# The latent attention's projection stage: tiles in turn, or a pipeline over three tiles

## The reference

```python
z = h @ lw['w_in']
c_q = rms_norm(z[..., :O_KVL], lw['g_q_lora'])
q = rms_norm(jnp.einsum('bsr,rhd->bshd', c_q, lw['w_uq']), lw['g_mla_qn'])        # 8 heads of 96
q = jnp.concatenate([q[..., :QK_NOPE], apply_rope(q[..., QK_NOPE:], cos, sin)], axis=-1)
latent = jnp.concatenate([rms_norm(z[..., O_KVL:O_KR], lw['g_kv_lora']), z[..., O_KR:O_DIL]], axis=-1)
...
k_nope = jnp.einsum('btr,rhd->bthd', c_kv, w_uk)      # 8 heads of 64
inv = lax.rsqrt((sum(k_nope ** 2) + sum(kr ** 2)) / QK_DIM + EPS)
k_nope = k_nope * (inv[..., None] * g_kn[:QK_NOPE])
kr = apply_rope(kr * g_kn[QK_NOPE:], cos, sin)        # 32 wide, times inv of each head
v = jnp.einsum('btr,rhd->bthd', latent[..., :KV_LORA], lw['w_uv'])
```

## Time and profile before

| | us |
|---|---|
| time, median of 3 executions (lowest to highest) | 4498.88 (4493.37 to 4502.63) |
| span of the profiled execution; no other time of it is recorded | 4461.3 |
| start of the tile loop's first product | 131.32 |
| start of the next stage's first product | 272.77 |
| TensorE busy over the whole span | 3866.2 (87%) |
| VectorE busy over the whole span | 2746.1 (62%) |
| ScalarE busy over the whole span | 1193.5 (27%) |

### The profile page before, as it was taken

One profiled execution on the slowest core, in us unless ns is written; L12 is line 12 of the kernel. 1 busy time (PEld: TensorE's weight loads), 2 busy tenths in 40 slices (PEclk: granted clock), 3 DMA queues, 4 the chain that ended last, 5 costly groups with the idle time before them and its releaser, 6 DMA issues.

```text
span 4461.3 us, 43547 instructions
## 1 busy us (share of the span) xinstructions
PE 3866.2 (87%) x14598; PEld 2550.7 (57%) x14598; DVE 2746.1 (62%) x6469; ACT 1193.5 (27%) x3201; POOL 861.8 (19%) x717
## 2 busy tenths in 40 slices
PE   7789879999995699977999677879999999899986
PEld 5458357798984588865444344434444445454443
DVE  1665535352345311236999997766779766976876
ACT  2356333232222101122222367621111111111111
POOL 0000000100000000001333323333333333343332
PEclk8889869997697599988999889999999999999997
DMA  4000200312114311125888879999999999999997
GB/s 152 5 2 1 55 38 22 117 45 85 60 48 152 105 43 43 62 92 194 310 316 328 326 306 354 384 418 414 413 398 379 414 412 410 373 394 414 389 357 286
DMA packets 252635, 1016.82 MB, mean 228 GB/s; under 512 B 25434, under 2 KB 100594, under 8 KB 167426
## 3 DMA queue, kind: packets, MB, share of 16 engines
q0 software_dynamic: 101520, 723.10, 40.9%
q1 hardware_dynamic: 130722, 280.49, 17.1%
q10 hardware_dynamic: 20176, 10.49, 0.8%
HBM read 964.74 MB, written 49.25 MB: 227 GB/s over the span
## 4 chain that ended last, share of the span: by engine, by line
PE 26%; DVE 15%; DMA 11%; issue 2%; ACT 2%; POOL 0%; SPq 0%; ACTq 0%; DVEq 0%
PE banks L2357 9%; PE banks L2343 8%; DMA ff_room<-in_v 8%; DVE ff_rows L2006 4%; PE banks L2332 4%; PE banks L2280 2%; DVE ff_acc L1972 2%; DMA gates_dram<-ff_room 1%; PE banks L2225 1%; DMA ff_rows<-in_uv,pk_expert 1%; DVE pk_eq L1662 1%; DVE pk_axes L1667 1%; DVE mx_x L2032 1%; PE banks L2304 1%; DVE pk_besti L1641 1%
## 5 line engine op out<-in xcount | busy, mean ns | idle before, releaser
L1904 POOL DMA_INDIRECT ff_rows<-in_uv,pk_expert x640 | 806.0, 1259 | 1507.6 <-DVE ff_acc L1972 828.4
L2006 DVE CUSTOM_DVE_ANT_0 ff_rows<-ff_rows,ff_h_row 128x1024 f32<-128x1024 f32 x648 | 766.4, 1220 | 43.9 <-DMA ff_rows<-in_uv,pk_expert 42.0
L2357 PE MATMUL banks<-ff_room,mx_x 128*128 128x512 f32 x1536 | 703.1, 609 | 59.0 <-DVE mx_x L2047 32.5
L2343 PE MATMUL banks<-mx_x,ff_room 128*128 128x384 f32 x2048 | 683.4, 487 | 10.9 <-ACT mx_x L2190 10.4
L2343 PEld LDWEIGHTS banks<-mx_x,ff_room 128*128 128x128 f32 x2048 | 389.3, 190 | 310.3 <-issue 73.5
L2332 PE MATMUL banks<-ff_rows,o_mla_tops 128*128 128x512 f32 x904 | 445.5, 642 | 138.3 <-ACT o_mla_tops L2100 134.7
L2357 PEld LDWEIGHTS banks<-ff_room,mx_x 128*128 128x128 f32 x1536 | 297.6, 195 | 420.6 <-issue 359.0
L1972 DVE SCALAR_TENSOR_TENSOR ff_acc<-ff_rows,ff_a,ff_acc 128x1024 f32<-128x1024 f32 x388 | 498.6, 1285 | 7.2
L2332 PEld LDWEIGHTS banks<-ff_rows,o_mla_tops 128*128 128x128 f32 x904 | 178.7, 206 | 355.4 <-issue 198.0
L176 PE MATMUL banks<-d_w_high,h_high 128*128 128x512 f32 (+1 forms) x648 | 275.7, 425 | 30.7 <-DVE d_w_low L183 29.8
L2088 ACT ACTIVATE ff_gelu<-ff_dots 128x2 f32<-128x2 f32 x324 | 65.7, 203 | 822.8 <-DVE ff_dots L2006 822.5
(11 more groups left out here) (379 smaller groups left out, 5942.9 us busy)
## 6 DMA issues: line engine op xcount, KB each, us to landing
ff_room<-in_uT SPq DMA_DIRECT2D x128, 512.0 KB
ff_room<-in_v SPq DMA_DIRECT2D x128, 512.0 KB
gates_dram<-ff_room SPq DMA_DIRECT2D x6, 4096.0 KB, 16.6
mx_x<-gates_dram SPq DMA_DIRECT2D x128, 192.0 KB
d_w<-in_w_dil POOLq DMA_DIRECT2D x9, 2048.0 KB, 12.7
d_w<-in_w_ada POOLq DMA_DIRECT2D x32, 512.0 KB, 4.7
ff_room<-in_w_pq SPq DMA_DIRECT2D x32, 512.0 KB
ff_rows<-in_uv,pk_expert POOLq DMA_INDIRECT x640
```

What stands on the lines that cost most here:

```text
L1904: pool.indirect_dma_start(out=rows[r][:, :], out_offset=None, in_=IN["uv"][:, :], in_offset=bass.IndirectOffsetOnAxis(ap=at, axis=0))\
L2006: ins = dve.tensor_tensor_reduce(rows[r][:, 0:D], rows[r][:, 0:D], h_row[i % 2][:], 1.0, 0.0, ALU.mult, ALU.add, dots[:, B % RB, j:j + 1])
L2343: ins = pe.matmul(SD[:, 0:ND], u[e % 4][:, k, :], hd[:, k, :], start=(k == 0), stop=(k == KD - 1))
L2357: ins = pe.matmul(Y[j][:, half], ad[e % 2][:, j * P:(j + 1) * P], v[e % 4][:, half_rows[half]], start=(e == 0), stop=(e == NK - 1))
```

## The change

The tile loop of `stage_mla_project` is written in another order. Two projections are done ahead of the loop, and turn t of TensorE's queue is: latent of t turned, queries of t-1 turned, K and V of t, `project(t + 2)`, keys of t-1 turned. ScalarE's turn: `ckT` of t, root of the keys of t-1, root of the queries of t, queries of t-1 copied to QT, K and its squares and V of t, the copies behind the projection of t+2, keys of t-1 copied to KT. VectorE's turn: latent of t scaled, key squares of t-1 summed, query squares of t summed, rope key of t rotated, keys of t-1 normed, queries of t normed and rotated. After the last turn the last tile's key part and transposes follow. The copies to QT move from VectorE to ScalarE, and the order of k and q in the banks X0 and X1 is turned round. Buffers: q three, squares of q two, k and its squares two, latent four, statistics four, rope key two; the squares and the inverse root of the q latent ahead of the loop share memory with the squares of q and with k.

```diff
+        q3 = [sb(f"q{i}", [P, MH, QK]) for i in range(3)]
+        qsq2 = [sb(f"qsq{i}", [P, MH * QK]) for i in range(2)]
+        k2 = sb("k", [P, 2 * MH * QK])
+        ksq2 = [sb(f"ksq{i}", [P, MH, NOPE]) for i in range(2)]
+        lat = [sb(f"lat{i}", [P, LAT]) for i in range(4)]
...
+        st = sb("stats", [P, 4, 7, MH])
+        krr2 = sb("krr", [P, 2, 1, ROPE])
...
+        sq = [qsq2[i][:, 0:2 * CH].rearrange("p (m n) -> p m n", m=2) for i in range(2)]
+        inv = k2[:, 0:TOK]
...
+        def stats(t):
+
+            return [st[:, t % 4, i] for i in range(7)]
...
+                    sp.dma_start(dst, lat[t % 4][0:n, :]).then_inc(lat_out[t % 4], 16)
...
-                def turn_heads(t, x, mm, copied, fin):
+                def turn_q(t):
...
-                    pe.wait_ge(fin, t + 1)
+                    pe.wait_ge(s["q_fin"], t + 1)
...
-                        if fin is s["q_fin"]:
-                            pe.wait_ge(s["kT_copy"], 2 * t + half + 1)
-                        elif t:
-                            pe.wait_ge(s["qT_copy"], 2 * t - 1 + half)
+                        if t:
+                            pe.wait_ge(s["kT_copy"], 2 * t - 1 + half)
...
+                def turn_k(t):
+                    n = TILES[t][1]
+                    pe.wait_ge(s["k_fin"], t + 1)
+                    for half, bank in ((0, X0), (1, X1)):
+                        pe.wait_ge(s["qT_copy"], 2 * t + half + 1)
...
                 project(0)
+                project(1)
                 for t, (t0, n) in enumerate(TILES):
                     pe.wait_ge(s["lat"], t + 1)
                     if t:
                         pe.wait_ge(s["trc"], t)
-                    pe.transpose(TR[:, 0:n], lat[t % 2][0:n, 0:KVL], c.ident[0:n, 0:n]).then_inc(s["tr"], 1)
+                    pe.transpose(TR[:, 0:n], lat[t % 4][0:n, 0:KVL], c.ident[0:n, 0:n]).then_inc(s["tr"], 1)
+                    if t:
+                        turn_q(t - 1)
...
-                    if t + 1 < len(TILES):
-                        project(t + 1)
-                    turn_heads(t, kf, s["kT_mm"], s["kT_copy"], s["k_fin"])
-                    turn_heads(t, qs, s["qT_mm"], s["qT_copy"], s["q_fin"])
+                    if t + 2 < NT:
+                        project(t + 2)
+                    if t:
+                        turn_k(t - 1)
+                turn_q(NT - 1)
+                turn_k(NT - 1)
 
...
+                def copies(t):
+
+                    n = TILES[t][1]
+                    one = stats(t)[6]
+                    if t >= 3:
+                        act.wait_ge(s["qT_mm"], 2 * (t - 2))
+                    for half, bank in ((0, A), (1, B)):
+                        act.wait_ge(s["q_mm"], 2 * t + half + 1)
+                        hs = slice(half * HB, (half + 1) * HB)
+                        src = bank[0:n, 0:HB * QK].rearrange("p (h d) -> p h d", d=QK)
+                        act.activation(q_of(t)[0:n, hs, :], src, ACT.Copy).then_inc(s["q_copy"], 1)
+                        if t >= 2 and half == 0:
+                            act.wait_ge(s["q_ss"], t - 1)
...
+                    act.wait_ge(s["kv_mm"], t + 1)
+                    if t >= 4:
+                        act.wait_ge(s["tr"], t - 3)
+                        act.wait_ge(s["k_fin"], t - 3)
+                        act.wait_ge(lat_out[t % 4], 16 * (t // 4))
+                    act.activation(lat[t % 4][0:n, :], KV[0:n, 0:LAT], ACT.Copy).then_inc(s["kv_copy"], 1)
...
+                def turned(t, mm, dst, done):
+                    t0, n = TILES[t]
+                    for half, bank in ((0, X0), (1, X1)):
+                        act.wait_ge(mm, 2 * t + half + 1)
+                        act.activation(dst[:, half * HB:(half + 1) * HB, :],
+                                       bank[0:QK, :].rearrange("p (h q) -> p h q", q=P)[:, :, 0:n],
+                                       ACT.Copy).then_inc(done, 1)
...
+                copies(0)
+                copies(1)
                 for t, (t0, n) in enumerate(TILES):
...
                     act.wait_ge(s["tr"], t + 1)
                     act.activation(ckT[:, 0:n], TR[:, 0:n], ACT.Copy).then_inc(s["trc"], 1)
-
+                    if t:
+                        root(t - 1, stats(t - 1)[3], stats(t - 1)[4], s["k_ss"], s["k_root"])
+                    root(t, stats(t)[0], stats(t)[1], s["q_ss"], s["q_root"])
+                    if t:
+                        turned_q(t - 1)
                     act.wait_ge(s["kn_mm"], t + 1)
-                    if t:
-                        act.wait_ge(s["kT_mm"], 2 * t)
+                    if t >= 2:
+                        act.wait_ge(s["kT_mm"], 2 * (t - 1))
+                        act.wait_ge(s["k_ss"], t - 1)
...
+                    if t + 2 < NT:
+                        copies(t + 2)
+                    if t:
+                        turned_k(t - 1)
+                root(NT - 1, stats(NT - 1)[3], stats(NT - 1)[4], s["k_ss"], s["k_root"])
+                turned_q(NT - 1)
+                turned_k(NT - 1)
...
+                def key_squares(t):
...
+                    dve.wait_ge(s["kn_copy"], 2 * t + 2)
+                    c.vstep(dve, dve.tensor_reduce(ss_k[0:n], ksq2[t % 2][0:n], AX.X, ALU.add))
+                    dve.tensor_scalar(ss_k[0:n], ss_k[0:n], one[0:n, 3:4], None, ALU.add).then_inc(s["k_ss"], 1)
+
+                def keys(t):
+                    n = TILES[t][1]
...
+                    normed_rows(dve, c, k_of(t)[0:n, :, 0:NOPE], ss_k[0:n], root_k[0:n], inv_k[0:n],
+                                c.rows[:, R_KN:R_KN + NOPE], NOPE, s["k_root"], tn, None)
+                    dve.tensor_tensor(k_of(t)[0:n, :, NOPE:QK], krr2[0:n, t % 2].to_broadcast([n, MH, ROPE]),
+                                      inv_k[0:n].unsqueeze(2).to_broadcast([n, MH, ROPE]),
+                                      ALU.mult).then_inc(s["k_fin"], 1)
...
                 for t, (t0, n) in enumerate(TILES):
...
                     dve.wait_ge(s["kv_root"], t + 1)
                     dve.wait_ge(s["kv_copy"], 2 * t + 2)
                     c.vstep(dve, dve.reciprocal(one[0:n, 2:3], one[0:n, 1:2]))
                     dve.scalar_tensor_tensor(out=L[0:n, 0:KVL], in0=L[0:n, 0:KVL], scalar=one[0:n, 2:3],
                                              in1=c.rows[0:n, R_KVL:R_KVL + KVL], op0=ALU.mult,
                                              op1=ALU.mult).then_inc(s["lat"], 1)
-
+                    if t:
+                        key_squares(t - 1)
+                    dve.wait_ge(s["q_copy"], 4 * t + 4)
+                    dve.tensor_reduce(ss_q[0:n], qsq_of(t)[0:n], AX.X, ALU.add).then_inc(s["q_ss"], 1)
                     c.vstep(dve, dve.tensor_tensor(krr[0:n, 0], L[0:n, KVL:LAT],
                                                    c.rows[0:n, R_KN + NOPE:R_KN + QK], ALU.mult))
                     rotate(dve, c, krr[0:n], krr[0:n], c.rot[:, 0, t], tmp)
-
+                    if t:
+                        keys(t - 1)
+                    qs = q_of(t)
                     normed_rows(dve, c, qs[0:n], ss_q[0:n], root_q[0:n], inv_q[0:n],
                                 c.rows[:, R_QN:R_QN + QK], QK, s["q_root"], tn, None)
                     rotate(dve, c, qs[0:n, :, NOPE:QK], qs[0:n, :, NOPE:QK], c.rot[:, 0, t], tmp,
                            s["q_fin"])
-
...
+                key_squares(NT - 1)
+                keys(NT - 1)
```

More of the change, by code:

```diff
@@ L348, in stage_mla_project @@
     HB = MH // 2
+    NT = len(TILES)
     with ExitStack() as ctx:
@@ L356, in stage_mla_project, with q_of, qsq_of, k_of @@
         zq = sb("zq", [P, 2, TOK])
[L357 to L363, removed]
+        q3 = [sb(f"q{i}", [P, MH, QK]) for i in range(3)]
[3 more added lines that the diff above has]
+        lat = [sb(f"lat{i}", [P, LAT]) for i in range(4)]
         junk = sb("junk", [P, LAT])
-        st = sb("stats", [P, 8, MH])
-        krr = sb("krr", [P, 1, ROPE])
+        st = sb("stats", [P, 4, 7, MH])
+        krr2 = sb("krr", [P, 2, 1, ROPE])
         tmp = sb("tmp", [P, 4, MH, RH])
         ckT = sb("ckT", [P, P])
-        names = ("w_in zq zcopy zsq zsum root cq cq_free q_mm q_copy kv_mm kv_copy q_ss q_root kv_root lat tr "
-                 "trc kn_mm kn_copy v_mm v_copy k_ss k_root q_fin k_fin kT_mm kT_copy qT_mm qT_copy lat_out").split()
+        sq = [qsq2[i][:, 0:2 * CH].rearrange("p (m n) -> p m n", m=2) for i in range(2)]
+        inv = k2[:, 0:TOK]
+        names = ("w_in zq zcopy zsq zsum root cq q_mm q_copy kv_mm kv_copy q_ss q_root kv_root lat tr "
+                 "trc kn_mm kn_copy v_mm v_copy k_ss k_root q_fin k_fin kT_mm kT_copy qT_mm qT_copy").split()
         s = {t: c.sem("mp_" + t) for t in names}
-        lat_out = [s["lat_out"], c.sem("mp_lat_out1")]
+        lat_out = [c.sem(f"mp_lat_out{i}") for i in range(4)]
         A, B, KV, TR, KN, V, X0, X1 = c.ps
-        ss_q, root_q, inv_q = st[:, 0], st[:, 1], st[:, 2]
-        ss_k, root_k, inv_k = st[:, 3], st[:, 4], st[:, 5]
```

(36 more changed lines are left out.)

56 lines of the change are left out of this document (18 added, 38 removed).

## The result

| us | kernel before | changed kernel |
|---|---|---|
| time, median (lowest to highest), 14 runs each | 4470.4 (4443.8 to 4502.6) | 4437.4 (4424.0 to 4454.8) |
| span of the profiled execution | 4461.3 | 4443.7 (its own time 4445.5) |
| first product of the tile loop | 131.32 | 155.83 |
| first product of the next stage | 272.77 | 253.19 |
| tile loop and barrier | 141.45 | 97.36 |

The ratio of the times is 0.9914, 95% interval 0.989 to 0.9939: 0.86% faster, and of the 4498.9 us that I started from, that is 38.7 us (27 to 49). The two medians lie 33.0 us apart, within that interval. The forecast was 38, and with an interval of 22 us that it came so close is luck in part. The median of 4437.4 us lies outside my range all the same, since the kernel before takes 4470 us in 14 runs, and not the 4498.9 of the first three of them.

The account below looks back on a forecast made before the run. It took the tile loop to be bound by a serial ring of waits across engines, 15.67 us a turn, with the clock falling to half. Its terms summed to 39.7 us saved, 38 taken from 4498.9, giving 4461 us, range 4452 to 4478.

Parts of the forecast that it names:

- the 37.6 us up to the median of 4498.9 us: Whole kernel: difference between the profiled span of 4461.3 us and the median time, assumed not to change.
- my sum: Tile loop and barrier: turn-by-turn total putting the next stage's first product at 233.1 instead of 272.77, 39.7 us less.
- my upper bound of 44.6: Tile loop: gain if VectorE alone set the pace, without any wait after its first query part.
- waits not placed: Tile loop: half a microsecond more in each of seven turns would leave a gain of 36 us; 38 taken.
- The turn of 9.65: TensorE in the tile loop: 9.23 us of work at full clock, .3 of stall and .1 for hops.
- The wait for X0: TensorE's query transposes wait until ScalarE has copied keys out of the bank; a stall of about .3 us.
- (a): Tile loop: projections two tiles ahead take the sum chain from before the transpose; cost a longer start, project(1) 4.92 us.
- (b): Tile loop: QT copies moved to ScalarE take 1.28 us a turn off VectorE, leaving 9.03, and add 1.08 to ScalarE.
- (c): Tile loop: key part of t-1 beside query part of t; TensorE's turn 9.23 us plus one wait, 9.65 taken.
- (d): Tile loop: added waits lie at least a turn back; VectorE waits for the key root, with 1.7 us slack.
- the rival that it falls once a turn: Tile loop: TensorE's clock still drops each turn, costing 2.5 us in seven turns, 17 us; 4478 us, chance 0.11.
- ScalarE's queue: Tile loop: ckT copy late in ScalarE's in-order queue, TensorE's turn 11.8 us, 13 us more; 4474 us, chance 0.07.

Follow-up runs that it names:

- one_ahead: Changed kernel with projections one tile ahead instead of two; loop and barrier 98.5 us, turn 9.48, one execution 4449.2 us.
- qt_vector: Changed kernel with the QT copies put back on VectorE; loop and barrier 104.2 us, turn 9.94, one execution 4410.9 us.
- both: Changed kernel plus five unused products in the first stage, ScalarE copying keys ahead of the latent chain; 4420.7 us, 0.9892 of the kernel before.
- warm_before: Kernel before plus four unused products per tile while TensorE waits for the latent; loop and barrier 129.6 us, one execution 4467.8 us.
- keys_copied_first: Changed kernel with only ScalarE's order edited, keys copied ahead of the latent chain; 4427.8 us, 0.988 of the kernel before, loop 94.9.
- keys_with_tile: Changed kernel with each tile's key part in its own turn; loop and barrier 116.2 us, turn 11.22, one execution 4461.8 us.
- root_earlier: keys_with_tile with ScalarE's query root moved ahead of the query copies to QT; loop and barrier 113.0 us, turn 11.22, one execution 4441.6 us.
- after_again: Changed kernel run again, unedited; 4433.5 us, 0.9924 of the kernel before, loop and barrier 98.7 us.

## Why the prediction was right or wrong

The step that failed is the first: "I set the 37.6 us up to the median of 4498.9 us as fixed". What lies around a span is 1.8 us (4445.5 against 4443.7). The other 36 us was the distance between one execution, profiled, and the median of three others, and both came from a scatter of 60 us that I took for none. The forecast of 4461 us is 4498.9 less the gain; taken from the 4470.4 that the kernel before takes in 14 runs, the same 38 us give 4432, and 4437.4 was measured. Another 25 runs of the kernel before gave 4471.8, so the first three were high ones of this scatter.

The gain was right within its interval, with errors in it that partly cancel:

- *Its size in time*: 38 forecast, 38.7 measured by the ratio (27 to 49). *In the trace*: loop and barrier 101.8 by my sum (141.45 less 39.7), 97.4 to 98.9 measured, so 42.6 to 44.1 us saved, just under my upper bound of 44.6. Of the 3.1 us between 101.8 and 98.7, of the loop whose first products took 5.49 us and not 4.25 (5.29 in my rows), 1.8 lie in five turns, .9 behind them and .4 in front. I then took 38 instead of 39.7 for waits not placed; the only one beyond the sum is .4 us more for X0. So the 38 fit the time's 38.7 better than the loop's 43 by luck.
- *The turn of 9.65*: 9.25. The wait for X0 is .74 where I had .3: the latent chain has the key transposes for cover, and these take .87 from start to next start, not the 1.08 of their row; and TensorE starts .72 us after ScalarE begins the first key copy (194.86 to 195.58), not .54. The same error the other way made each of three terms too long by .1 to .2: query transposes .89 for 1.08, w_kv 2.17 for 2.34, key transposes .87. The row of the key transposes says 1.04 where the next row starts after .87, so where work follows, starts to starts count.
- *(a) projections two ahead*: I placed no price on the second tile. It is worth nothing that can be told: 98.5 us without it, 97.4 to 98.9 with it (one_ahead).
- *(b)* worth 6.9 us (qt_vector), from VectorE as said. The cost was somewhat too high: 9.03 and 1.28 give 10.3, 9.94 was measured. VectorE's turn without the copies is 8.74 (in `both`: key squares .86 for .94, query squares .86 for .95, key part 2.03 for 2.12), and the copies take 1.20 from start to next start.
- *(c)* the split: 1.16 us a turn with both roots earlier on ScalarE, 1.97 without.
- *(d)* VectorE's wait for the key root: expected half a microsecond, .54.
- *The clock*: the rival that it falls once a turn is out, 1.00 from 176 to 230 us. 2.8 us of transposes and waits between the projections left the clock full. What the Trainium skill states of transposes (TensorE: Matmul & The Clock Gate, Part 4: PE-mode transpose) did no harm here; whether it is so, no run shows, since none was made with transposes alone. That part of the gain is the clock is shown by warm_before: 12 of 44.
- *ScalarE's queue* as a rival did not come true at its price of 2.5 us a turn, and TensorE waits for ckT once in the middle turns, .3 us. But the .74 us for X0 is a wait through that queue: keys_copied_first won .5 a turn there. keys_with_tile and root_earlier lost .8 a turn to the same kind of wait.

## What to carry to other kernels

A span plus a constant is not a time: look at how far single executions lie apart before an absolute number is given, and forecast the difference. In a pipeline over several engines, write the turn of each engine's queue from starts to starts, and then look at the smallest instructions: a root of .3 us behind a copy that waits for a projection held a turn at 11.2 us, and moving only one of two such roots left the turn as it was. How many tiles ahead one works mattered far less than freeing the buffers (31 of the 44 us were there with TensorE's old order, QT copies and clock included) and that two chains no longer stand in each other's queue.

## What the runs showed of the hardware that I had not expected

In these traces a granted clock of 1.00 at the start is no evidence of full speed. From 20 to 60 us it reads 1.00 in the changed kernel's trace, and there 16 products with w_ada took 3.42 us; it still reads 1.00 from 90 to 110 us, where TensorE does nothing at all. In after_again it reads 1.00 from 20 to 60 us too, and the same products take first 3.42 and then 1.85. That the two durations are the two levels of the clock is argued from the factor, not shown.

The first stage, in which TensorE is busy 40.0 of the 40 us from 20 to 60 in both cases, took two speeds in the same program: its loop over w_ada ran at 6.85 or at 3.53 us a turn, in one execution at first the one and then the other. Five dense products ahead of it gave the faster in all three profiled executions (starts at 136.5, 136.2 and 135.2, against 131.0 to 156.1 in the eleven without, of which two had the faster from its first turn on). The dilated attention did the like, .54 against .91 of the clock over 120 us in two kernels that have it unchanged. The first moves the loop's start by 25 us, the second the mix by 47: as much as this change.
